# Two fused transformer blocks on one core: each weight block with one 512-column and one 256-column matmul in place of three of 256, and the two halves of the sum added at eviction

## The reference

```python
def first_block(x, ...):                 # once
    proj = rmsnorm(x) @ w_in + b_in      # q k v o i f, conv b c h, two gates
    hm = mlstm_chunkwise(q, k, v, i, f)  # 4 heads; normed, times sigmoid(o)
    y_m = hm @ w_branch_m
    y_c = (cb * causal_dwconv(cc * ch, conv_w)) @ w_branch_c
    h = x + (sigmoid(gm) * y_m + sigmoid(gc) * y_c) @ w_out
    u = causal_dwconv(rmsnorm(h) @ w_up, ffn_conv_w, ffn_conv_b)   # D_FF = 5504
    h = h + (silu(gate) * val) @ w_down
    return rmsnorm(h)
x = x + rms_norm(gla_mixer(rms_norm(x), ...))   # 4 heads, gated linear attention
x = x + rms_norm(mla_mixer(rms_norm(x), ...))   # 16 heads, latent attention with rope
```

## Time and profile before

| what | value |
|---|---|
| time, three runs | 2305.95, 2307.69, 2307.79 us; median 2307.69 |
| span of the profiled execution | 2306.9 us |
| TensorE matmul busy | 2207.6 us, 96% |
| VectorE, ScalarE, GpSimd busy | 1288.3, 1214.1, 287.2 us |
| DMA | 393.8 MB, mean 171 GB/s, 16 engines busy 47% |
| chain that ended last | PE 75%, issue 16%, POOL 3%, DVE 3%, ACT 2% |
| wup | 717 to 1218 us; VectorE busy 314, ScalarE 332 |
| wdown | 1218 to 1463 us |
| mla | 1973 to 2196 us; VectorE busy 135, ScalarE 131 |

### The profile page before, as it was taken

The page is one execution under the profiler, slowest core; times in us unless marked ns, Lnnn a source line. Parts: engine busy times, 40 slices in busy tenths (PEclk is TensorE's granted clock), DMA queues, the critical chain, the costliest instruction groups (busy, mean ns, idle before and its releaser), DMA issues.

```text
span 2306.9 us, 47015 instructions
## 1 busy us (share of the span) xinstructions
PE 2207.6 (96%) x17592; PEld 2165.1 (94%) x17592; DVE 1288.3 (56%) x1529; ACT 1214.1 (53%) x1666; POOL 287.2 (12%) x349
## 2 busy tenths in 40 slices
PE   6999999999998999999999999799999988999996
PEld 5999999999997999999999999789999978899996
DVE  5555564444446666666665555555555556655534
ACT  5444445544445666666664444555555444555643
POOL 2000000010112000000001000200100113121111
PEclk7999999999998999999999999899999999999998
DMA  3544545445453555555555555344444433444443
GB/s 144 181 166 166 180 166 185 183 177 192 174 186 138 182 182 182 182 182 182 182 182 201 206 212 197 131 158 171 166 172 174 179 130 132 163 161 145 145 173 118
DMA packets 54923, 393.77 MB, mean 171 GB/s; under 512 B 6097, under 2 KB 6225, under 8 KB 7522
## 3 DMA queue, kind: packets, MB, share of 16 engines
q1 hardware_dynamic: 54432, 392.19, 47.3%
q10 hardware_dynamic: 450, 1.02, 0.1%
HBM read 391.09 MB, written 2.10 MB: 170 GB/s over the span
## 4 chain that ended last, share of the span: by engine, by line
PE 75%; issue 16%; POOL 3%; DVE 3%; ACT 2%; DMA 0%; DVEq 0%; POOLq 0%; ACTq 0%
PE acc L536 22%; PE acc L538 22%; PE acc L537 22%; PE tok L573 2%; PE tok L574 2%; PE tok L575 2%; POOL n_lo L1816 1%; POOL sumsq L1805 1%; PE att L591 1%; POOL sumsq_g L1807 1%; DVE rstd L1302 0%; DVE normed L1316 0%; POOL x L1829 0%; POOL probs L1971 0%; ACT n_hi L897 0%
## 5 line engine op out<-in xcount | busy, mean ns | idle before, releaser
L1294 DVE TENSOR_TENSOR w_lo<-raw,w_hi 128x1024 fp32r<-128x1024 f32 x740 | 912.2, 1246 | 764.4 <-ACT w_hi L874 762.5
L536 PE MATMUL acc<-n_hi,w_hi 128*128 128x256 f32 x3488 | 1002.3, 287 | 42.9 <-POOL n_lo L1816 35.5
L537 PE MATMUL acc<-n_lo,w_hi 128*128 128x256 f32 x3488 | 994.7, 285 | 0.0
L538 PE MATMUL acc<-n_hi,w_lo 128*128 128x256 f32 x3488 | 994.7, 285 | 0.0
L874 ACT ACTIVATE w_hi<-raw 128x1024 fp32r<-128x1024 f32 x740 | 771.5, 1054 | 369.3 <-DMA raw<-stream_in 153.9
L536 PEld LDWEIGHTS acc<-n_hi,w_hi 128*128 128x128 f32 x3488 | 677.5, 194 | 48.1 <-issue 39.9
L537 PEld LDWEIGHTS acc<-n_lo,w_hi 128*128 128x128 f32 x3488 | 677.8, 194 | 0.5
L538 PEld LDWEIGHTS acc<-n_hi,w_lo 128*128 128x128 f32 x3488 | 677.4, 194 | 0.0
L536 PE MATMUL acc<-f_hi,w_hi 128*128 128x256 f32 x688 | 193.6, 281 | 0.0
L537 PE MATMUL acc<-f_lo,w_hi 128*128 128x256 f32 x688 | 193.6, 281 | 0.0
L538 PE MATMUL acc<-f_hi,w_lo 128*128 128x256 f32 x688 | 193.6, 281 | 0.0
(11 more groups left out here) (305 smaller groups left out, 3001.6 us busy)
## 6 DMA issues: line engine op xcount, KB each, us to landing
raw<-stream_in SPq DMA_DIRECT2D x370, 1024.0 KB, 4.8
x<-x_in SPq DMA_DIRECT2D x4, 512.0 KB, 7.5
out<-x SPq DMA_DIRECT2D x4, 512.0 KB, 2.6
v_bias<-v_bias_in ACTq DMA_DIRECT2D x1, 512.0 KB, 8.7
par<-params_in ACTq DMA_DIRECT2D x1, 287.0 KB, 5.5
pos_i<-positions_in ACTq DMA_DIRECT2D x1, 128.0 KB, 6.8
gk<-gk_in ACTq DMA_DIRECT2D x1, 68.0 KB
```

The source lines that it names most:

```text
L536: nc.tensor.matmul(out, w_hi[:, s, wc], hi[:, k, :], start=first, stop=False)
L537: nc.tensor.matmul(out, w_hi[:, s, wc], lo[:, k, :], start=False, stop=False)
L538: return nc.tensor.matmul(out, w_lo[:, s, wc], hi[:, k, :], start=False, stop=last)
L1294: nc.vector.tensor_tensor(w_lo[:, s, :], raw[:, s, :], w_hi[:, s, :].bitcast(fp32), ALU.subtract).then_inc(lo_ready, 1)
```

## The change

The high and low activations now lie side by side for each tile (`n_both[:, k, 0:2, :]`, 512 contiguous columns), and `n_hi`, `n_lo` are views of it. A block is two matmuls: w_hi with all 512 columns (high's product in columns 0:256 of the bank, low's in 256:512) and w_lo with the high 256 columns added to the first half. The halves are summed at eviction. ScalarE moves the second half to `side` in SBUF (`side_of`), VectorE adds the first half (`fold`) and frees the bank. What was a function of the sum (sigmoid, silu, scale and bias, squares) is now computed from the folded tile in SBUF, after the `split` of that step. In wout and wdown VectorE adds both halves to x in two chained adds. `unit_done` counts two per unit. In mla each half tile of a pair unit has a bank of its own.

```diff
@@ TensorE
+            def tile(o, s, c, both, k, first, last):
                 wc = slice(c * P, (c + 1) * P)
-                nc.tensor.matmul(out, w_hi[:, s, wc], hi[:, k, :], start=first, stop=False)
-                nc.tensor.matmul(out, w_hi[:, s, wc], lo[:, k, :], start=False, stop=False)
-                return nc.tensor.matmul(out, w_lo[:, s, wc], hi[:, k, :], start=False, stop=last)
+                def high(start, stop):
+                    return nc.tensor.matmul(o[:, :], w_hi[:, s, wc], both[:, k, :, :].rearrange("p a t -> p (a t)"),
+                                            start=start, stop=stop)
+                def low():
+                    nc.tensor.matmul(o[:, 0:T], w_lo[:, s, wc], both[:, k, 0, :], start=False, stop=False)
+                if first:
+                    high(True, False)
+                    low()
+                    return None
+                low()
+                return high(False, last)
...
+            def pair_tiles(i, j, use, k0, spare=0):
                 pe.wait_ge(c_ready, k0 + A_TILES)
                 s = unit("mla", i, j)
+                for m in range(2):
+                    o = bank(m, "mla", i, use)
+                    for k in range(A_TILES):
+                        last = tile(o, s, m * A_TILES + k, c_both, k0 + k, k == 0, k == A_TILES - 1)
+                    last.then_inc(unit_done, 1 + m * spare)
@@ ScalarE
+            def side_of(b, rows=slice(0, P), **how):
+                nc.scalar.activation(side[rows, b, :], acc[b][rows, T:2 * T], ACT.Identity, **how)\
+                    .then_inc(side_ready[b], 1)
@@ ScalarE, wup, step j
                         unit_is_done("wup", i, j)
-                        if n == 0:
-                            act.wait_ge(fsilu_ready, FREE + i)
-                        else:
-                            act.wait_ge(fact_ready, FREE + i)
-                        nc.scalar.activation((f_gate, f_val)[n][:, :], acc[1 - n][:, 0:T], ACT.Identity,
...
-                        nc.scalar.activation(f_pre[:, n, :], acc[1 - n][:, 0:T], ACT.Copy)\
-                            .then_inc(acc_taken[1 - n], 1)
+                        side_of(1 - n)
                     if j == 2:
                         act.wait_ge(ftap_ready, 2 * i + 1)
-                        act.wait_ge(fact_ready, FREE + i)
-                        nc.scalar.activation(f_silu[:, :], f_gate[:, :], ACT.Silu)\
+                        nc.scalar.activation(f_gate[:, :], f_gate[:, :], ACT.Silu)\
                             .then_inc(fsilu_ready, 1)
                     split("wup", i, j)
+                    if j in (1, 3):
+                        n = j // 2
+                        taken(act, 1 - n, "wup", i, 0)
+                        act.wait_ge(fact_ready, FREE + i)
+                        nc.scalar.activation((f_gate, f_val)[n][:, :], f_pre[:, n, :], ACT.Identity,
+                                             bias=par_ffn[:, i, 4 * n + 3:4 * n + 4],
+                                             scale=par_ffn[:, i, 4 * n + 2:4 * n + 3]).then_inc(flin_ready, 1)
@@ ScalarE, gla, step j
-                        nc.scalar.activation(o_sg[:, n, :], acc[n % 2][:, 0:T], ACT.Silu)\
-                            .then_inc(acc_taken[n % 2], 1)
+                        side_of(n % 2)
...
+                    split("gla", i, j)
+                    if j in (17, 19, 21, 23):
+                        n = (j - 17) // 2
+                        taken(act, n % 2, "gla", i, 2 + n // 2)
+                        nc.scalar.activation(o_sg[:, n, :], o_sg[:, n, :], ACT.Silu).then_inc(osg_ready, 1)
@@ ScalarE, mla, step j
-                        nc.scalar.activation(qn[:, 2 * n:2 * n + 2, :], acc[0][:, :], ACT.Copy)\
-                            .then_inc(acc_taken[0], 1)
...
+                    if j < 5:
+                        for m in range(2):
+                            unit_is_done("mla", i, j, m)
+                            side_of(m)
...
+                    split("mla", i, j)
                     if j in (9, 11, 13, 15):
...
+                        taken(act, 1 - n % 2, "mla", i, 5 + n // 2)
+                        nc.scalar.activation(a_gate[:, n, :], a_gate[:, n, :], ACT.Silu).then_inc(agate_ready, 1)
@@ VectorE
+            def fold(out, b, name, i, use, rows=slice(0, P)):
+                side_done(dve, b, name, i, use)
+                nc.vector.tensor_tensor(out, acc[b][rows, 0:T], side[rows, b, :], ALU.add)\
+                    .then_inc(acc_taken[b], 1)
@@ VectorE, residual of wout and wdown
-                            nc.vector.tensor_tensor(x[:, 2 * i + m, :], acc[1 - m][:, 0:T],
+                            chain.link(nc.vector.tensor_tensor(x[:, 2 * i + m, :], acc[1 - m][:, 0:T],
+                                                               x[:, 2 * i + m, :], ALU.add))
+                            nc.vector.tensor_tensor(x[:, 2 * i + m, :], acc[1 - m][:, T:2 * T],
                                                     x[:, 2 * i + m, :], ALU.add)\
@@ VectorE, wup, step j
+                        fold(f_pre[:, n, :], 1 - n, "wup", i, 0)
+                    split("wup", i, j)
+                    if j in (1, 3):
                         u = (f_gate, f_val)[n]
-                        taken(dve, 1 - n, "wup", i, 0)
+                        dve.wait_ge(flin_ready, 2 * i + n + 1)
                         src = f_pre[:, n, :]
...
-                    split("wup", i, j)
@@ VectorE, mla, step j
-                        nc.vector.tensor_copy(kn[:, 2 * n:2 * n + 2, :], acc[1][:, :])\
-                            .then_inc(acc_taken[1], 1)
+                    if j < 4:
+                        for m in range(2):
+                            fold((qn, kn)[j % 2][:, 2 * (j // 2) + m, :], m, "mla", i, j)
+                    if j == 4:
+                        for m in range(2):
+                            dve.wait_ge(qprod_ready, 2 * i)
+                            fold(q_r[:, m, :], m, "mla", i, j)
```

More of the change, by code:

```diff
@@ L40 @@
 PHASES = [
[L41 to L53, removed]
+    ("gates", 1, 2, 1, 0, 0, 1, 0),
+    ("mix", M_HEADS, 24, 5, 5, 1, 5, 5),
+    ("merge", KT // 2, 12, 4, 4, 0, 4, 4),
+    ("wout", KT // 2, 4, 1, 1, 0, 0, 0),
+    ("wup", F_TILES, 4, 1, 1, 0, 1, 1),
+    ("wdown", KT // 2, 12, 1, 1, 0, 0, 0),
+    ("rank", 1, 2, 0, 1, 0, 0, 1),
+    ("gla", G_HEADS, 24, 4, 4, 1, 4, 4),
+    ("glaout", KT // 2, 4, 1, 1, 0, 1, 1),
+    ("latent", 1, 16, 4, 4, 0, 4, 4),
+    ("krope", 1, 4, 1, 1, 0, 1, 1),
+    ("mla", A_HEADS // 4, 16, 7, 7, 1, 7, 7),
+    ("mlaout", KT // 2, 4, 1, 1, 0, 1, 1),
 ]
@@ L118, in program @@
         square = sb("square", [P, 2, T])
+        side = sb("side", [P, 2, T])
         sumsq = sb("sumsq", [P, T])
@@ L680, in _ @@
                 for m in range(2):
-                    o = bank(1 - m, "wdown", i, 0)[:, 0:T]
+                    o = bank(1 - m, "wdown", i, 0)
                     for n in range(6):
@@ L854, in _ @@
                 for m in range(2):
-                    feature_tile("mlaout", i, 2 * m, 1 - m, 0, mo_hi, mo_lo, ready=((molo_ready, 1),))
+                    feature_tile("mlaout", i, 2 * m, 1 - m, 0, mo_both, ready=((molo_ready, 1),))
             norm_sum("post1")
@@ L1155, in _ @@
                                 .then_inc(oghi_ready, 1)
-                    split("gla", i, j)
             def mixer_output(name, n, gain, to, flip):
@@ L1275, in _ @@
                                 .then_inc(mohi_ready, 1)
-                    split("mla", i, j)
             mixer_output("mlaout", "post1", "g_post1", y2, True)
@@ L1540, in _ @@
             last_splits("wdown", 12)
+            dve.wait_ge(rank_ones, 1)
+            fold(rank_rows[0:G_RANK, :], 1, "rank", None, 0, slice(0, G_RANK))
             split("rank", None, 0)
@@ L1634, in _ @@
                                                 ALU.subtract).then_inc(oglo_ready_dve, 1)
-                    split("gla", i, j)
+                    else:
+                        split("gla", i, j)
                 chain.done(G_HEADS)
@@ L1781, in _ @@
                 for j in range(4):
-                    split("mlaout", i, j)
+                    outputs_folded("mlaout", y2, i, j, True)
+                    for k in split_after(j, (1, 3)):
+                        split("mlaout", i, k)
+            for j in range(4):
+                outputs_folded("mlaout", y2, KT // 2 - 1, j, True)
             add_normed("post1", y2, 1)
```

385 lines of the change are left out of this document (209 added, 176 removed).

## The result

The changed kernel takes 2325.97 us (median of 4 runs, 2323.86 to 2327.40) against 2307.65 us (4 runs, 2305.95 to 2307.79): ratio 1.0081, interval 1.0066 to 1.0095. It is 0.8% slower, where 1.2% faster was forecast. The profiled span grew from 2306.9 to 2322.2 us, where 2279.9 was the sum.

The account below looks back on a forecast made before the run. TensorE was taken to bound the kernel: 2306.9 - 53.1 (blocks outside wup) + 1.3 (wup) + 14.4 (mla) + 1.7 + 1.5 + 3.8 + 3.4 (clock) = 2279.9 us span, so 2281 us; own range 2266 to 2297, eight in ten 2252 to 2304.

Parts of the forecast that it names:

- The cost of a block: All weight blocks: 346.7 ns instead of 360, one fixed part of 13.3 ns saved, 71.5 us over 5,360 blocks.
- The range's bounds of 333.3 and 360: Block price: 360 ns if the pair keeps all three fixed parts, 333.3 if the narrow one's is hidden.
- not cheaper, or only in part: Chance entry for blocks gaining nothing or less than claimed: 0.06, of which 0.02 the same and 0.04 slower.
- The mean round: wup: serial ScalarE and VectorE work per F tile, 10.95 or 12.36 us, mean 11.66, against TensorE's 11.09.
- the lead: wup: prepared weights run ahead, taken as 4.7 us; used up after some eight of 43 F tiles.
- The waits for folds and kr: mla: TensorE waits for banks, 3.2 us three times between iterations and +4.8 into iteration 0, together +14.4.
- two more stretches at half speed: Clock: extra matmul-free time brings two more drops to 1.2 GHz at 1.7 us each, +3.4 (0 to 7).
- The wait for og at the head of glaout: Last gla head to glaout: silu now stands after w_hi and its table load is not hidden, +1.5 us.
- The serial end of rank: End of rank: side copy and fold add 0.6 us, part of the +3.8 for serial ends.
- wup 18.3 + 1.3: wup: the 1,376 blocks' 18.3 us gain is lost, and the stage grows by 1.3 us.
- 1.7 + 1.5 + 3.8: Small terms: gain lost in existing waits +1.7; last gla head to glaout +1.5; serial stage ends +3.8 us.
- (3): Rival: the block does not get cheaper, the pair takes 360 ns and only costs stay, 2334 us; chance 0.06.

Follow-up runs that it names:

- the run of the matmuls alone: Kernel before with the new 512- and 256-column blocks but old evictions, high-weight by low-activation product left out, mla pair units keeping three matmuls: 2279.26 us, ratio 0.9880.
- the run on near and far operands: Changed kernel with other operands by stage, from the same or different parts of SBUF, results wrong, only matmul starts count: one run, 2155.34 us.
- both repairs: Changed kernel with wup's gate half one unit later and mla's pair units as before the change (one bank, three matmuls): 2288.97 us, ratio 0.9914.
- the run of widths in runs: Changed kernel with wup's gate later, mla's pair units in one bank, and feature tiles ordered eight wide, eight narrow, then eight narrow, eight wide: 2286.03 us, ratio 0.9910.
- The run of the eviction alone: Changed kernel with the wide matmul cut into two of 256 columns in all blocks except each tile's first, new eviction kept: 2347.54 us, ratio 1.0170.

## Why the prediction was wrong

**The cost of a block: the step that failed.** "Both widths pay 13.3 in the earlier trace rows, so I take 346.7." Two stretches of unmixed matmuls, both on n_hi and n_lo, were made into a law of an additive fixed part. The mixed pair costs 352.9 ns on n_both and 351.2 on the others. The saving was priced at 71.5 us over 5,360 blocks; the run of the matmuls alone has 30.1, of which 7.0 in wup. Outside wup that is 23.1 instead of 53.1, and this alone turns 2280 into 2310. It also had before's blocks at 360 everywhere, while those on the arena's buffers took 356.1. What spoke against it stood in the trace of before: 232.4 ns in mla's token tiles. The range's bounds of 333.3 and 360 held the value; I gave "not cheaper, or only in part" 0.06.

The Trainium skill's page "TensorE: Matmul & The Clock Gate" (section "Wait — 56ns, not 53.3ns?") has columns over 1.2 GHz exactly at the lower clock, and 2.5 ns more than columns over 2.4 GHz at the higher. The trace agrees with the first (426 to 427 ns wide and 213 to 214 narrow at a granted 0.50 in the run on near and far operands) and not with the second: 13.3 ns on near operands, and 10 to 22 in the other sequences. The section of the Trainium skill that the prediction names, "Back-to-back issue gap", gives the 2.5 ns for single matmuls in isolation, and it was held against a stream.

**wup: mechanism right, size off.** Onset after eight tiles, the wait for f_pre, and tiles that alternate (11.2 and 12.3 in the trace) came as forecast. The mean round was 11.72, not 11.66 (+2.6 us in 43 tiles), the first tile took 19.3 us where it had taken 16.7 (+2.5, also in the run of the matmuls alone), and the lead gave some 1 us less: +7.6 instead of +1.3.

**mla: mechanism right, sizes off.** The waits for folds and kr are 12.1 us against 1.3 for kn, +10.8, where +14.4 was forecast; they stand where they were expected, with 2.4 and 3.2 us in iteration 0 and 1.9 in the others. The clock made up for it and more: two more stretches at half speed were allowed for (+3.4, at most 7), and in mla alone there are five more, +8.5. Over the whole span the time at half clock went from 98.1 to 121.1 us, which is 11.5 us lost.

**Small terms.** The wait for og at the head of glaout, given +1.5, grew by 2.1 (1.5 to 3.5 us). The serial end of rank, given 0.6, shows as 0.4 in the pause behind it (7.7 to 8.1 us). But the stage rank itself, which was given nothing, takes 3.9 us more: its waits for n_both are 4.35, 1.19 and 0.64 us after the first, against one of 1.96 before, and with the old eviction it takes 12.2 us, so about 3 us come with the new eviction. No run shows by which step.

**Sum.** The forecast is -71.5 for the blocks and +44.4 for the new eviction (wup 18.3 + 1.3, mla 14.4, clock 3.4, and 1.7 + 1.5 + 3.8). The run of the matmuls alone has -30.1 for the blocks, and the kernel after lies 45.3 above that run. So 41.4 of the 42.3 us between 2279.9 and 2322.2 are the blocks. That the eviction's total came out within a microsecond is luck, for its parts did not: wup 14.6 instead of 19.6, mla 20.4 instead of some 18.6 with the clock, rank 3.1 instead of nothing, glaout 3.0 instead of 1.5, the pauses 4.7 instead of 3.8, and mix 2.4 less.

**Rivals.** None came alone. It was a part of (3), the block cheaper by 37 to 53% of the claim (4.9 and 7.1 of 13.3 ns), on top of the forecast's own losses.

## What to carry to other kernels

Before an instruction's price is carried to a new sequence, read it in every stage where that form stands; a second stretch that disagrees says that the price belongs to the place or the neighbours. An eviction that needs two engines in turn can be made cheap (10 us of 2289 with both repairs), but it must not stand in a chain with the work that feeds the bound engine: give each step to a later slot than the one that makes its input, and keep one bank a unit where the next unit wants the bank at once. A few waits of 2 to 3 us can cost as much again in clock.

## What the runs showed of the hardware that was not expected

- In these kernels the spacing of matmuls at full clock depends on where the two operands lie and on the widths around: 226.7 (wide) and 120 (narrow) among their own kind with both operands in one part of SBUF, about 232 and 118.7 with them in two, 352.9 for an alternating pair of near ones. Why, the traces don't show.
- After a change of width, or a pause, the first five spacings of wide matmuls on near operands are 233, 235, 229, 232 and 231 ns in the mean, and from the sixth or so on it is 226.7 (the run of widths in runs).
- A GpSimd addition that begins while VectorE is at a w_lo takes longer. The 64 additions of sumsq took 722 to 747 ns before. In the kernel after 35 still take 722 to 748, and 29, all in glaout and mlaout, 1652 to 1665: exactly these begin inside a w_lo (1.22 us, raw and w_hi from SBUF), since the new eviction moved the two together. The run of the eviction alone has the same 35 and 29, that of the matmuls alone none. f_lo went the other way: all 43 began inside a w_lo before (988 to 1094 ns), none after (732 to 748). No run changed this alone. VectorE and GpSimd in glaout, then GpSimd in wdown, kernel after:

```profile
1802.92 1.22 DVE L1319 TENSOR_TENSOR w_lo<-raw,w_hi 128x1024 fp32r<-128x1024 f32 x1
1803.07 1.67 POOL L1896 TENSOR_TENSOR sumsq<-sumsq,square 128x256 f32<-128x256 f32 x1 [4.12 <-ACT square L915]
...
1261.18 0.75 POOL L1896 TENSOR_TENSOR sumsq<-sumsq,square 128x256 f32<-128x256 f32 x1 [13.63 <-ACT square_g L917]
```
